# A hybrid layer on one core: heads from half tile 28 in eight steps, no key pages between the projections, ten weight rests on GpSimd

## The reference

```python
xn = rms_norm(x, norm1_g)
u_pool, h_b, h_c, h_x, q, k, v, f_logit = split(xn @ w_in)        # 2048 -> 4 tiles of pooling, 12 of convolution, 24 of q, k, v
y_pool = causal_pool_mix(u_pool, ...)                             # windows 2, 4, 8, 16, then a 128x128 product per group
y_conv = h_b * causal_dwconv(h_c * h_x, ...)                      # 3 taps
q, k = rms_norm(q per head), rms_norm(k per head)
y_att = fox_attend(q, k, v, cumsum(log_sigmoid(f_logit + b_f)))   # 8 heads of 128; the samples attend to 32 pages of 128 rows each
x = x + concat(rms_norm(y_pool), rms_norm(y_conv), rms_norm(y_att)) @ w_o
a, gate = split(rms_norm(x, norm2_g) @ w_up)
x = x + (silu(causal_dwconv(a) + b) * gate) @ w_down              # d_ff = 5632
```

## Time and profile before

| | us |
|---|---|
| median of 3 runs (2840.59 to 2846.02) | 2841.31 |
| the profiled execution | 2837.32 |
| its span | 2835.7 |
| TensorE busy | 2607.2 (92%) |
| VectorE busy | 1424.3 (50%) |
| ScalarE busy | 737.4 (26%) |
| GpSimd busy | 169.4 (6%) |
| transfers | 524.03 MB, mean 185 GB/s |

### The profile page before, as it was taken

The page is one execution under the profiler, slowest core; times in us unless marked ns, Lnnn a source line. Parts: engine busy times, 40 slices in busy tenths (PEclk is TensorE's granted clock), DMA queues, the critical chain, the costliest instruction groups (busy, mean ns, idle before and its releaser), DMA issues.

```text
span 2835.7 us, 50766 instructions
## 1 busy us (share of the span) xinstructions
PE 2607.2 (92%) x19729; PEld 2336.7 (82%) x19729; DVE 1424.3 (50%) x5630; ACT 737.4 (26%) x1029; POOL 169.4 (6%) x343
## 2 busy tenths in 40 slices
PE   6878898898985599979999999999999999999998
PEld 3777677777773255549999999999999999999998
DVE  5787776767655942234434343434343434343433
ACT  5222123333431311133222222222222222222221
POOL 0100111111112121200000000000000000000000
PEclk8888989999997799989999999999999999999999
DMA  8678999998989697753222222222222222222221
GB/s 298 219 253 313 353 332 338 341 350 314 360 287 341 220 371 247 267 178 119 90 90 90 90 90 90 90 90 90 93 101 99 96 90 90 90 90 90 90 90 64
DMA packets 272564, 524.03 MB, mean 185 GB/s; under 512 B 16535, under 2 KB 182268, under 8 KB 271012
## 3 DMA queue, kind: packets, MB, share of 16 engines
q1 hardware_dynamic: 218717, 365.71, 37.4%
q0 software_dynamic: 40304, 142.46, 13.7%
q10 hardware_dynamic: 13303, 12.62, 1.3%
HBM read 501.58 MB, written 17.50 MB: 183 GB/s over the span
## 4 chain that ended last, share of the span: by engine, by line
PE 61%; DMA 2%; DVE 2%; issue 1%; ACT 1%; POOL 0%; POOLq 0%; DVEq 0%; ACTq 0%
PE ps L740 61%; DMA t_r<-in_cache_v 1%; DMA t_wraw<-in_w_o 1%; DVE t_xl L1681 1%; DVE t_r L1852 0%; DVE t_stg L1737 0%; PE ps L743 0%; DVE t_wl L1681 0%; ACT t_xh L1267 0%; DVE t_work L1681 0%; DVE t_stg L2024 0%; ACT t_wh L1267 0%; POOL out_conv_prompt L539 0%; POOL out_conv_sample L539 0%; POOLq L542 0%
## 5 line engine op out<-in xcount | busy, mean ns | idle before, releaser
L740 PE MATMUL ps<-t_xh,t_wh 128*128 128x260 f32 (+1 forms) x4352 | 1078.3, 299 | 36.4 <-DVE t_wlr L1681 21.4
L740 PE MATMUL ps<-t_xl,t_wh 128*128 128x260 f32 (+1 forms) x4352 | 1051.1, 293 | 0.0
L740 PEld LDWEIGHTS ps<-t_xh,t_wh 128*128 128x128 f32 x4352 | 743.3, 192 | 169.5 <-issue 116.2
L1267 ACT ACTIVATE t_wh<-t_wraw 128x1024 fp32r<-128x1024 f32 x376 | 398.5, 1060 | 1465.9 <-PE ps L740 1392.0
L1681 DVE TENSOR_TENSOR t_wl<-t_wraw,t_wh 128x1024 fp32r<-128x1024 f32 x296 | 362.4, 1225 | 824.9 <-ACT t_wh L1267 824.9
L740 PEld LDWEIGHTS ps<-t_xl,t_wh 128*128 128x128 f32 x4352 | 742.5, 192 | 10.2 <-issue 1.2
L740 PE MATMUL ps<-t_xh,t_wl 128*128 128x260 f32 (+1 forms) x3072 | 676.9, 293 | 0.0
L1852 DVE CUSTOM_DVE_ANT_0 t_r<-t_r,t_work 128x128 f32<-128x128 f32 x2048 | 455.0, 287 | 205.0 <-DMA t_r<-in_cache_k 188.5
L740 PEld LDWEIGHTS ps<-t_xh,t_wl 128*128 128x128 f32 x3072 | 487.4, 189 | 12.0
L740 PE MATMUL ps<-t_xh,t_wlr 128*128 128x260 f32 x1280 | 374.1, 292 | 0.0
L740 PE MATMUL ps<-t_hh,t_wh 128*128 128x260 f32 x1408 | 283.0, 282 | 3.4 <-issue 3.4
(11 more groups left out here) (305 smaller groups left out, 1250.2 us busy)
## 6 DMA issues: line engine op xcount, KB each, us to landing
t_r<-in_cache_k SPq DMA_DIRECT2D x256, 512.0 KB, 6.5
t_r<-in_cache_v POOLq DMA_DIRECT2D x256, 512.0 KB, 6.7
t_wraw<-in_w_up SPq DMA_DIRECT2D x44, 2048.0 KB, 8.0
t_wraw<-in_w_down SPq DMA_DIRECT2D x22, 2048.0 KB, 7.7
t_wraw<-in_w_in SPq DMA_DIRECT2D x21, 2048.0 KB, 14.2
t_wraw<-in_w_o SPq DMA_DIRECT2D x11, 2048.0 KB, 11.3
scr_x<-t_r POOLq DMA_DIRECT2D x1, 4160.0 KB, 20.0
t_work<-in_x_prompt SPq DMA_DIRECT2D x4, 1024.0 KB, 6.6
```

Source lines behind the costliest of these rows:

```text
L740: return pe.matmul(out, lhsT, rhs, start=start, stop=stop)
L1267: return act.activation(out, in_, ACT.Copy)
```

## The change

- **Heads.** `HEAD0` is 28 and `STAGES` 8: head `h` begins in slot 28 + 6h and ends in slot 35 + 6h, head 7 in slot 77. The transposes move from stage 5 to stage 6, one slot behind the division, the product with v to stage 7. k rows are now made in stage 3 and v rows in stage 4. The sum of q's squares goes to bank 3 instead of 6. Head 7's output is stored and loaded back as the others are.
- **Key pages.** Up to 4 in the first two slots of each sequence, then 3: ten slots to a sequence instead of eleven. None in slots 80 to 83; the last six stand in slots 84 and 85, for which SP waits until the outputs are loaded back. Before slot 28 there are now 84 key pages (76 before), in slots 28 to 79 166 (151), in the gap 0 (12), behind it 6 (17). Value pages: 28 (26), 128 (128), 16 (14), 84 (88). The tables of small steps (`MISC`) follow.
- **GpSimd.** It makes the rests of chunks 8 to 17 (`POOL_RESTS`) in its slots 5 to 14, instead of VectorE. VectorE waits for them before it makes that of chunk 18.
- **The gap.** In slot 80 the convolution, its squares and the total of the attention squares; in slot 81 the total of the convolution squares, the rows of the convolution and the rests of the first four output chunks; in slots 82 and 83 all eight `mix_pair`.
- **Stores of rows.** Rows are laid out so that the stores of the pooling state and of the samples' keys and values take one transfer each instead of four or eight (15 in all instead of 32).

```diff
-HEAD0 = 32
-STAGES = 7
+HEAD0 = 28
+STAGES = 8
+POOL_RESTS = range(8, 18)
@@ page_slots
-            take = min(3, PAGES - done)
+            if CHUNKS <= at < OUT0:
+                at = OUT0
+            take = min(4 if done < 8 else 3, PAGES - done)
@@ GpSimd
+            def tile_rest(c):
+                pool.wait_ge(w_hi, c + 1)
...
+                pool.wait_ge(w_lo, c)
+                pool.tensor_tensor(kept, raw, wh[:, c % 4, :].rearrange("p (k n) -> p k n", k=8).bitcast(F32), ALU.subtract)\
+                    .then_inc(w_lo, 1)
             for s in range(SLOTS):
+                if s + 3 in POOL_RESTS:
+                    tile_rest(s + 3)
                 value_loads(VALUES.get(s, []))
@@ SP
+                if s == OUT0:
+                    sp.wait_ge(y_loaded, 32)
@@ TensorE, rows_of and head
-                if stage == 0:
-                    rows_of(h, 0)
...
-                    rows_of(h, 1)
-                if stage == 5:
+                    rows_of(h, 0)
+                if stage == 4:
+                    rows_of(h, 1)
+                if stage == 6:
                     pe.wait_ge(h_pn, h + 1)
-                    pe.wait_ge(h_e, h + 1)
...
-                if stage == 6:
+                if stage == 7:
                     pe.wait_ge(h_pC, 4 * h + 4)
@@ TensorE, slots
+                if s == CHUNKS:
+                    pe.wait_ge(h_pC, 4 * HEADS)
+                    mix_total(2, 14, msum[2], 2)
                 if s == CHUNKS + 1:
                     conv_rows()
-                if s == CHUNKS + 2:
-                    pe.wait_ge(h_done, HEADS)
-                    mix_total(2, 14, msum[2], 2)
                     mix_total(1, 16, msum[1], 5)
@@ VectorE, slots
-                if s + 3 >= 4 and s + 3 < CHUNKS:
+                if s + 3 >= 4 and s + 3 < CHUNKS and s + 3 not in POOL_RESTS:
+                    if s + 3 == POOL_RESTS.stop:
+                        dve.wait_ge(w_lo, POOL_RESTS.stop)
                     tile_rest(s + 3)
...
+                if s == CHUNKS - 1:
+                    mix_sum(13)
+                if s == CHUNKS:
+                    mix_sum(14)
+                    mix_sum(15)
                 if s == CHUNKS + 1:
-                    for n in range(13, 16):
-                        mix_sum(n)
-                    mix_pair(0)
-                    mix_pair(2)
-                if s == CHUNKS + 2:
                     dve.wait_ge(h_O, HEADS)
                     dve.wait_ge(h_stored[1], 16 * HEADS)
-                    weight_rest(0, CHUNKS)
...
+                    dve.wait_ge(y_stored, 16 * 14)
+                    for c in range(4):
+                        weight_rest(0, CHUNKS + c)
...
+                if s == CHUNKS + 2:
+                    for t in range(0, 8, 2):
+                        mix_pair(t)
                 if s == CHUNKS + 3:
-                    for t in range(4, 16, 2):
+                    for t in range(8, 16, 2):
                         mix_pair(t)
```

More of the change, by code:

```diff
@@ L194, in hybrid_layer_kernel @@
         qsk = sb("qsk", [P, 3 * HEADS * DEC])
-        qS, sm, kSn = [qsk[:, 64 * i:64 * (i + 1)].rearrange("p (h b) -> p h b", h=HEADS) for i in range(3)]
+        qS, sm = [qsk[:, 64 * i:64 * (i + 1)].rearrange("p (h b) -> p h b", h=HEADS) for i in range(2)]
+        kSn, vSn = [qsk[:, at:at + 64].rearrange("p (b h) -> p h b", h=HEADS) for at in (128, 64)]
         qg8 = qsk[0:DEC, 0:HD]
@@ L420, in square_place @@
         def square_place(n):
-            return stg[:, 0, 0:SEQ] if n < 13 else sq_late
+            return stg[:, 0, 0:SEQ] if n < 14 else sq_late
         def sum_place(n):
@@ L1008, in head @@
                     pe.wait_ge(h_ln, h + 1)
-                    if h == 0:
+                    if h:
+                        pe.wait_ge(h_done, h)
+                    else:
                         pe.wait_ge(x_log, 1)
@@ L1121, in _ @@
                     mix_total(0, 4, sums_pool, 5)
-                at_head = head_stages(s)
-                value_pages(late[:2])
-                for h, stage in at_head:
-                    if stage != 5:
-                        head(h, stage)
+                if s == CHUNKS:
+                    pe.wait_ge(h_pC, 4 * HEADS)
+                    mix_total(2, 14, msum[2], 2)
                 if s == CHUNKS + 1:
                     conv_rows()
-                if s == CHUNKS + 2:
-                    pe.wait_ge(h_done, HEADS)
-                    mix_total(2, 14, msum[2], 2)
                     mix_total(1, 16, msum[1], 5)
+                value_pages(late[:2])
+                for h, stage in head_stages(s):
+                    head(h, stage)
                 if s == OUT0:
@@ L1471, in prompt_head @@
                     act.activation(sqs, sqs, ACT.Exp, scale=-0.5).then_inc(h_rs, 1)
-                    if h:
-                        mix_square(5 + h, yhead)
+                if stage == 2 and h:
+                    mix_square(5 + h, yhead)
                 if stage == 3:
-                    head_rows(h, 1)
+                    head_rows(h, 0)
                 if stage == 4:
@@ L1481, in prompt_head @@
                     last.then_inc(h_e, 1)
-                if stage == 5:
+                    if h == 0:
+                        act.wait_ge(m_stored1, 16)
+                    else:
+                        act.wait_ge(h_O, h)
+                    head_rows(h, 1)
+                if stage == 6:
                     if h:
@@ L1572, in _ @@
                         mix_square(12 + g, ymix[:, 4 + g, 0:SEQ])
+                if s == CHUNKS + 1:
+                    mix_rstd(3, 5, 512, msum[1])
                     act.wait_ge(r_full, 2)
@@ L1994, in prompt_head @@
             def prompt_head(h, stage):
+                if stage == 3 and h:
+                    mix_sum(5 + h)
                 if stage == 2:
-                    if h:
-                        mix_sum(5 + h)
                     dve.wait_ge(h_rs, h + 1)
```

102 lines of the change are left out of this document (51 added, 51 removed).

## The result

The changed kernel takes 2808.25 us (median of four runs, 2805.51 to 2811.12), the kernel before 2840.95 beside it (2837.56 to 2846.02). The ratio is 0.9884, 95% interval 0.9863 to 0.9904: 33 us faster, where 72 were forecast. The time is inside the range, near its slow end. The profiled execution has a span of 2804.0 us, against 2835.7.

A forecast was written before the change was run, and what follows sets the result against it. The prediction held the heads' stage bound by TensorE and DMA in turn, not VectorE's work. Pooling -3, heads -21, gap -41 and output projection -7 summed to -72 us, from 2841.3 to 2769 us, range 2722 to 2816.

The forecast's parts named there:

- Pooling, -3 forecast: Slots 5 to 14: rests leaving VectorE save 12.2 us, more key pages cost 8.6; -3 us, ends -12 and +12.
- A GpSimd rest is shown nowhere ... I take 2.4: Pooling: a weight rest on GpSimd was taken at 2.4 us, between 1.22 and 3.5.
- the third rival: Pooling: VectorE stands while GpSimd makes the rests, so pooling +12 and 2784 us in all; chance 0.15.
- five more key pages are done by slot 17: 5 x 1.71 = 8.6 us: Pooling: the work that the new page table adds to VectorE by slot 17, 8.6 us.
- Heads, -21 forecast: Heads' stage, slots 28 to 79: 550.7 us becomes 530 despite 15 more key pages; ends +23 and -61.
- L2012 waits: Heads: TensorE's six waits for VectorE's scaling of the probabilities, 35.4 us, go because the transposes move one slot later.
- I take 363: Heads: the transfer rate rises from 335 to 363 GB/s once TensorE's stalls are gone.
- held by TensorE and DMA in turn, not by VectorE's work: Heads' stage before the change: TensorE and DMA limit it; VectorE is busy only 381.19 of 550.7 us.
- Gap, -41 forecast: Half tile 79 to output chunk 2: without key pages 66.5 us against 107.9; ends -52 and -33.
- Output projection, -7 forecast: Behind the gap: fewer key and value pages recover a third of TensorE's 20.7 us idle; -7 us, 0 to -15.
- the first rival: Heads: the path stays at 335 GB/s, so the stage costs +23 and the kernel takes 2813 us; chance 0.15.
- The fourth: Heads: key pages behind weights land too late, delaying chunk rests; slower, 2864 us at 25 us landing; chance 0.04 with like stalls.

The follow-up runs named there:

- R: The kernel before with the ten weight rests moved to GpSimd and nothing else: 2851.7 us, ratio 1.0025.
- the one with eight pieces: The kernel before with the ten weight rests on GpSimd, each cut into eight subtractions of 128 columns: 2848.97 us, ratio 1.0026.
- K: The kernel before with the new table of key pages and nothing else: 2836.16 us, ratio 0.9978.
- one page ahead: SP issues one key page per four slots before waiting for the weight buffer: 2809.3 us in the kernel before, 2780.01 in the changed with rests on VectorE.
- H: The changed kernel with the old key page table and rests on VectorE, leaving eight-stage heads, new gap order and fewer row stores: 2816.0 us, ratio 0.9899.
- K, H: The changed kernel with its ten weight rests back on VectorE: 2799.57 us, ratio 0.9855.
- the run with the extra pages late: The changed kernel with rests on VectorE and three key pages per slot until slot 34, four in a round's first two slots only from there: 2781.8 us, ratio 0.9788.

## Why the prediction was wrong, and where it was right

The sum was -72 and came to -32 (the four terms as measured; -33 in the medians). By its terms:

**Pooling, -3 forecast, +26 measured: the term that failed**, beyond its own ends of -12 and +12. About 22 of the 29 us are GpSimd's rests. *"A GpSimd rest is shown nowhere ... I take 2.4"* was right in the size (2.34 to 2.49 us) and wrong in the effect: the third rival's mechanism, which had 0.15, is what happens. With R the pooling is longer by 10.3, 9.7 and 9.9 us in three pairs of kernels (by 4.4 in the one with eight pieces); its place in the sum was a gain of 12.2 us of VectorE's work. The other 7 us are pages. The step *"five more key pages are done by slot 17: 5 x 1.71 = 8.6 us"* leaves out the three pages more of slots 22 and 23; eight come to 13.7 us, and K costs 13.6 to 15.8. That the price held over the stage is partly chance: the two pages of slots 2 and 3 cost 7.6 us for 3.4 of work, the six others 8 for 10, and with one page ahead all eight cost 20.6. It was also misread that GpSimd's *"wait for VectorE's eight first rests is met"*: GpSimd stood 18.14 us for them. That did no harm, as its rest of chunk 8 was through at 125.91, where VectorE began it at 125.88 before.

**Heads, -21 forecast, -4 measured: the rate.** H alone takes 28.9 us off and K's fifteen pages put 24.7 back (25.3 between H and K, H); the two add up. The mechanism, L2012 waits that vanish and let the rate rise, was right: 335 to 352 GB/s in H, with DMA at 0.97. The step *"I take 363"* was 11 to 13 GB/s too high, and 192 MB at 350 instead of 363 are 20 us. And *"held by TensorE and DMA in turn, not by VectorE's work"* is wrong: halving VectorE's products took more off than halving the bytes. The four key buffers join the two, and VectorE's time per page counts in that loop though it is busy for only 405.74 of 546.8 us. How much of the stage each part of the loop holds is open; more buffers weren't tried.

**Gap, -41 forecast, -38 measured.** The landing at 31.0 us (29 forecast), the pairs (21.7, 21.8), the reduction (11.6, 9.1) and the last 5.8 (6.6) came step by step. The landing is closer still by the forecast's own numbers: 12.8 MB less 2.1, with two value pages (1.0) and one head (0.3) more, is 12.0 MB and not 11.5, which is 31 us at 384 GB/s. The reduction is later by the 3.12 us wait for ScalarE, which the sum did not have. What the sum did not say is that the missing pages do it: K alone gives 30.0, H alone 0.6.

**Output projection, -7 forecast, -17 measured.** It lies outside the term's own ends (0 to -15). A third of TensorE's idle time was a guess, and low. As the FFN takes the same time in both, the gain is all in the output projection. K alone gives 12.0 us. A page there costs 1.1 us in K (eleven), 1.2 in the run with the extra pages late (nine) and 1.7 where fourteen came in.

**The rivals.** The rate stayed between the first rival's 335 and the forecast's 363. The fourth, chunk rests too late, shows in the heads in one wait of 4.9 us and no more. In the pooling, where the prediction did not look for it, it is what the two pages of slots 2 and 3 cost, and in the kernel before TensorE already stood 16.0 us for rests there, nearly all of it for those of chunks 7, 23 and 27. VectorE's key waits were to be no smaller than 188.5 us and are 157.1, because the 27.05 us wait of the gap was part of them and went; in the heads they stayed (114.5 us before, 117.4 after). The third rival's +12 for the pooling leaves out the 8.6 us of pages that its own baseline counts; with them the prediction's numbers give +20. With 20 us for the lower rate the rival (2784) comes to 2804, near the 2808 measured, but partly by luck: its pooling is 14 us short and its output projection 10 us long.

## What to carry to other kernels

Before work is moved beside an engine, look for what that engine's instructions do to the neighbour: an offload to GpSimd that saves 1.2 us and makes VectorE stand for 2.4 is a loss wherever VectorE is waited for. Put the price of moved work at the places where somebody waits for the engine behind it, not on its sum over a stage; here a 1.7 us page cost 1.1 to 2.0 us in most places, 2.5 in the gap and nearly 4 where it stood in the queue ahead of weights and of a page that a chunk rest waited for. When an engine answers late, look whether it worked or waited itself. A queue that waits for one buffer with the next loads behind it is worth a look before any larger rebuilding: one load in each group of four slots, moved ahead of the wait, gave as much as this whole change.

## What the runs showed of the hardware

- A key product of 0.28 us took 2.38 to 2.49 us beside a GpSimd subtraction of 2.34 to 2.56 us, in nine of ten cases of R, and 0.98 in one that began near the subtraction's end (2.36 to 2.50, and 1.67, in the changed kernel); beside pieces of mostly 0.45 to 0.59 us it took up to 0.57. So here the hold lasts one GpSimd instruction and no longer.
- GpSimd's subtraction of 128x1024 elements takes 2.4 us, VectorE's 1.22.
- One core's DMA moved 370 GB/s over 518 us, with the engines' share at 0.99, where the kernel kept the same bytes at 350.
